# Up half of the expert super-blocks by seven block products in place of eight, with weight sums on VectorE

## What is computed

```python
def expert_block(args):
    xb, e = args
    hid = jax.nn.silu(xb @ w_gate[e]) * (xb @ w_up[e])
    return hid @ w_down[e]
```

## Time and profile before

| | |
|---|---|
| timed runs | 1322.66, 1323.9, 1325.47 us; median 1323.9 us |
| span of the profiled execution, first to last instruction | 1321.3 us |
| TensorE busy | 1299.1 us, 98% of the span |
| VectorE busy | 360.1 us, 27% |
| DMA | 442.52 MB, mean 335 GB/s over the span |
| the item loop | from 444 to 1313 us |
| one item | 108.5 us |

### The profile page before, as it was taken

The page is one execution under the profiler, slowest core; times in us unless marked ns, Lnnn a source line. Parts: engine busy times, 40 slices in busy tenths (PEclk is TensorE's granted clock), DMA queues, the critical chain, the costliest instruction groups (busy, mean ns, idle before and its releaser), DMA issues.

```text
span 1321.3 us, 32549 instructions
## 1 busy us (share of the span) xinstructions
PE 1299.1 (98%) x14662; PEld 879.8 (67%) x14662; DVE 360.1 (27%) x539; ACT 246.4 (19%) x370; POOL 56.0 (4%) x50
## 2 busy tenths in 40 slices
PE   8999999999899999999999999999999999999998
PEld 8998899988767533555745655665574575566565
DVE  5875555554875401000000100100100010010011
ACT  5554544443743100000000000000000000000000
POOL 1001000000000320000000000000000000001600
PEclk9999999999999899999999999999999999999999
DMA  9866555565522899999999999999999999999992
GB/s 321 269 210 225 185 182 177 187 223 191 184 96 72 360 421 420 415 419 418 416 419 419 418 418 418 418 410 419 419 404 420 418 407 418 416 409 414 419 413 110
DMA packets 114199, 442.52 MB, mean 335 GB/s; under 512 B 9284, under 2 KB 55700, under 8 KB 83348
## 3 DMA queue, kind: packets, MB, share of 16 engines
q1 hardware_dynamic: 107904, 424.75, 81.5%
q10 hardware_dynamic: 4820, 11.53, 2.5%
q0 software_dynamic: 1344, 4.20, 0.8%
HBM read 434.12 MB, written 12.08 MB: 338 GB/s over the span
## 4 chain that ended last, share of the span: by engine, by line
PE 93%; DVE 3%; ACT 2%; issue 1%; DMA 0%; ACTq 0%; DVEq 0%
PE bank L1888 44%; PE bank L1900 22%; PE bank L1442 8%; PE bank L1444 8%; PE bank L1443 8%; PE bank L1689 1%; PE bank L1600 1%; DVE w_lo L916 1%; ACT w_hi L626 0%; PE bank L1865 0%; DMA const<-in_shape_constants 0%; ACT ht_hi L654 0%; PE bank L1744 0%; PE bank L1940 0%; DVE q_from L1100 0%
## 5 line engine op out<-in xcount | busy, mean ns | idle before, releaser
L1888 PE MATMUL bank<-more_ring,xT 128*32 128x512 f32 (+1 forms) x3456 | 341.0, 545 | 0.0
L1888 PEld LDWEIGHTS bank<-more_ring,xT 128*32 128x32 f32 x3456 | 164.2, 110 | 163.5 <-issue 84.4
L1888 PE MATMUL bank<-raw,xT 128*32 128x384 f32 (+1 forms) x2688 | 259.3, 532 | 0.7 <-DVE xT L1352 0.7
L1888 PEld LDWEIGHTS bank<-raw,xT 128*32 128x32 f32 x2688 | 122.4, 110 | 127.0 <-issue 76.6
L1411 DVE TENSOR_TENSOR e_hid<-e_silu,bank 128x384 f32<-128x384 f32 (+1 forms) x48 | 26.9, 616 | 542.3 <-PE bank L1888 542.3
L1900 PE MATMUL bank<-more_ring,hidT 128*32 128x256 f32 x3072 | 171.4, 379 | 0.0
L916 DVE TENSOR_TENSOR w_lo<-raw,w_hi 128x2048 fp32r<-128x2048 f32 x62 | 141.5, 2289 | 99.1 <-ACT w_hi L626 99.0
L1900 PEld LDWEIGHTS bank<-more_ring,hidT 128*32 128x32 f32 x3072 | 120.8, 110 | 46.4
L1442 PE MATMUL bank<-ht_hi,w_hi 128*128 128x256 f32 x464 | 129.4, 279 | 1.5 <-DVE ht_lo L930 1.5
L1900 PE MATMUL bank<-raw,hidT 128*32 128x256 f32 x2304 | 129.9, 379 | 0.0
L1444 PE MATMUL bank<-ht_hi,w_lo 128*128 128x256 f32 x464 | 128.9, 278 | 0.0
(11 more groups left out here) (284 smaller groups left out, 898.6 us busy)
## 6 DMA issues: line engine op xcount, KB each, us to landing
more_ring<-in_moe_w_up SPq DMA_DIRECT2D x64, 1024.0 KB, 16.2
more_ring<-in_moe_w_down SPq DMA_DIRECT2D x64, 1024.0 KB, 16.9
raw<-in_moe_w_gate SPq DMA_DIRECT2D x64, 768.0 KB, 15.5
more_ring<-in_moe_w_up SPq DMA_DIRECT2D x64, 768.0 KB, 15.8
raw<-in_moe_w_gate SPq DMA_DIRECT2D x48, 1024.0 KB, 16.1
raw<-in_moe_w_down SPq DMA_DIRECT2D x48, 1024.0 KB, 17.5
more_ring<-in_moe_w_gate SPq DMA_DIRECT2D x16, 1024.0 KB
raw<-in_hgrn_w_in SPq DMA_DIRECT2D x15, 1024.0 KB, 11.8
```

Source lines behind the costliest of these rows:

```text
L1888: ins = nc.tensor.matmul(out_banks[j][GTOK * c:GTOK * c + GTOK, 0:w], xT[:, j, kt, :], chunk[:, c], start=kt == 0, stop=kt == KT - 1)
```

## The change

For token groups 0 and 1 the up half of both super-blocks is computed in pairs of loads (k, k+1). With the token groups as block rows, the two loads as inner blocks and each load's columns cut in half, a pair is a 2 x 2 by 2 x 2 block product. It is formed by seven block products in place of eight: two take token and weight blocks as they are, one takes a token sum and a weight block, one a token block and a weight sum, and three take sums of both. Group 2 is computed as before, in two column halves. The token sums (`token_sums`) and the weight sums (`weight_sums`: four VectorE subtractions of 128 x 768 or 128 x 1024 for each pair) are new, as are the additions that put the seven partial results together (`up_columns`). The products need banks 3 to 7, so the down sums move to banks 1 and 2, where the next item's gate sums of groups 1 and 2 also stand: TensorE therefore begins an item with three loads' products of group 0 and waits for the copies of the last item's result before the other groups. `up_used` now counts a pair of up loads as one step, and `wait_used` and GpSimd's spreads go by that. The early results are fetched into `xs` and a new tile, since `early`'s place now holds the weight sums.

The core of the diff:

```diff
+FAST = (True, True)
...
+            def token_sums(done):
+
+                a11, a12, a21, a22 = (xT[:, j, k:KT:2, :] for j in range(2) for k in range(2))
+                s1, s2, s3, s4 = (xsum[:, i, :, :] for i in range(4))
+                nc.vector.tensor_tensor(s1, a21, a22, ADD).then_inc(xsum_ready, 1)
+                nc.vector.tensor_tensor(s3, a11, a21, SUB).then_inc(xsum_ready, 1)
...
+            def weight_sums(n, sup, pair):
...
+                nc.vector.tensor_tensor(t1, b12, b11, SUB).then_inc(sum_ready, 1)
+                free(2)
+                nc.vector.tensor_tensor(t3, b22, b12, SUB).then_inc(sum_ready, 1)
+                free(3)
+                dve.wait_ge(sum_ready, n * T_STEPS + (done + 1))
+                nc.vector.tensor_tensor(t2, b22, t1, SUB).then_inc(sum_ready, 1)
+                if pair:
+                    dve.wait_ge(up_used, n * UP_STEPS + (PHASE_END[2 * sup] + pair))
+                dve.wait_ge(sum_ready, n * T_STEPS + (done + 3))
+                nc.vector.tensor_tensor(t4, t2, b21, SUB).then_inc(sum_ready, 1)
+            def up_columns(n, sup):
...
+                nc.vector.tensor_tensor(s2, s1, piece("P6", b), ADD).then_inc(part_ready, 1)
+                nc.vector.tensor_tensor(e_hid[:, 0, lo], s1, piece("P2", b), ADD).then_inc(part_ready, 1)
...
+                    act.wait_ge(up_used, n * UP_STEPS + PHASE_END[2 * sup + 1])
+                    nc.scalar.activation(up_part[:, 0, 0:w // 2], piece("P1", w // 2), ACT.Copy).then_inc(first_copied, 1)
...
-                nc.scalar.activation(yb[:, 0:512], banks[6][0:CAP, :], ACT.Copy)
+                nc.scalar.activation(yb[:, 0:512], banks[1][0:CAP, :], ACT.Copy)
...
+            def fast_products(n, sup, pair):
...
+                def times(name, rows, columns, begin=True):
+                    dst, opens = piece(name, b), PLACES[name][2] and begin and pair == 0
+                    for c in range(4):
+                        ins = nc.tensor.matmul(dst[GTOK * c:GTOK * c + GTOK, :], rows, columns[:, c], start=opens,
+                                               stop=pair == PAIRS - 1, skip_group_check=True)
+                    return ins
+
+                times("P1", xT[:, 0, k, :], b11)
+                times("P2", xT[:, 0, k + 1, :], b21)
+                if pair == 0:
+                    pe.wait_ge(xsum_ready, n * 4 + 4)
+                times("P3", xsum[:, 3, pair, :], b22)
+                times("H1", xT[:, 2, k, :], b11)
+                times("H1", xT[:, 2, k + 1, :], b21, False)
+                times("H2", xT[:, 2, k, :], b12)
+                times("H2", xT[:, 2, k + 1, :], b22, False)
+                pe.wait_ge(sum_ready, n * T_STEPS + (done + 1))
+                times("P5", xsum[:, 0, pair, :], t1).then_inc(sum_used, 1)
+                pe.wait_ge(sum_ready, n * T_STEPS + (done + 2))
+                times("P7", xsum[:, 2, pair, :], t3).then_inc(sum_used, 1)
+                pe.wait_ge(sum_ready, n * T_STEPS + (done + 3))
+                times("P6", xsum[:, 1, pair, :], t2).then_inc(sum_used, 1)
+                pe.wait_ge(sum_ready, n * T_STEPS + (done + 4))
+                times("P4", xT[:, 1, k + 1, :], t4).then_inc(up_used, 1)
...
-                            ins = nc.tensor.matmul(banks[6 + j // 2][GTOK * c:GTOK * c + GTOK, 256 * (j % 2):256 * (j % 2) + 256],
+                            ins = nc.tensor.matmul(banks[1 + j // 2][GTOK * c:GTOK * c + GTOK, 256 * (j % 2):256 * (j % 2) + 256],
...
+                        for kt in range(AHEAD):
+                            loaded(kt)
+                            up_products(banks, kt, w, (0,))
+                        pe.wait_ge(yb_ready, n * 2 + 1)
+                        for kt in range(AHEAD):
+                            up_products(banks, kt, w, (1, 2))
+                        plain = range(AHEAD, KT)
...
+                    if FAST[sup]:
+                        for pair in range(PAIRS):
+                            loaded(i + 2 * pair)
+                            loaded(i + 2 * pair + 1)
+                            fast_products(n, sup, pair)
...
-                        pe.wait_ge(yb_ready, n * 2 + 1)
+                        pe.wait_ge(e_silu_ready, n * (2 * GRPS) + 2 * GRPS)
```

More of the change, by code:

```diff
@@ L49 @@
 SIGNALS = N_LOADS // 2
+FAST = (True, True)
+UP_USED, PHASE_END = [], []
+for _sup in range(2):
+    for _half in range(2):
+        _done = PHASE_END[-1] if PHASE_END else 0
+        _step = 2 if _half and FAST[_sup] else 1
+        UP_USED += [_done + kt // _step + 1 for kt in range(KT)]
+        PHASE_END.append(_done + KT // _step)
+UP_STEPS = PHASE_END[-1]
+PAIRS = KT // 2
+AHEAD = 3
+FAST_BEFORE = (0, PAIRS if FAST[0] else 0)
+T_STEPS = 4 * PAIRS * sum(FAST)
 def ring_offset(k):
@@ L153, in build_program @@
         with ExitStack() as over:
-            early = sb(over, "early", [P, TT, 2, D])
+            sums = sb(over, "sums", [P, 4, 4 * 256])
         ht_hi = sb(ctx, "ht_hi", [P, KT, T], f32r)
@@ L161, in build_program @@
         cols = sb(ctx, "cols", [P, 64])
+        with ExitStack() as over:
+            up_part = sb(over, "up_part", [P, 2, 256])
+            xsum = sb(over, "xsum", [P, 4, PAIRS, GTOK])
         gain_row = sb(ctx, "gain_row", [P, D])
@@ L251, in build_program @@
         s = ExitStack()
+        early_second = sb(ctx, "early_second", [P, TT, D])
         e_silu = sb(s, "e_silu", [P, GRPS, 512])
@@ L423, in build_program, with piece @@
         LO_FFN, LO_KV, LO_Q = 4, 8, 12
-        END_BANKS = [banks[1], banks[2], banks[5], banks[0]]
+        END_BANKS = [banks[3], banks[4], banks[5], banks[6]]
+        early = [xs[:, :, :], early_second[:, :, :]]
+        PLACES = {"P1": (3, 0, True), "P2": (3, 1, False), "P3": (4, 0, True), "H1": (5, 0, True), "H2": (5, 1, False),
+                  "P5": (4, 1, False), "P7": (6, 0, True), "P6": (6, 1, False), "P4": (7, 0, True)}
+        def piece(name, width):
+            bank, half, _ = PLACES[name]
+            return banks[bank][:, width * half:width * half + width]
         TURN0 = TURN_ATT
@@ L599, in _ @@
                     at = bass.IndirectOffsetOnAxis(ap=early_slot[:, t, i:i + 1], axis=0)
-                    nc.gpsimd.indirect_dma_start(out=early[:, t, i, :], out_offset=None, in_=slot_rows, in_offset=at).then_inc(fetched[t][i], 16)
+                    nc.gpsimd.indirect_dma_start(out=early[i][:, t, :], out_offset=None, in_=slot_rows, in_offset=at).then_inc(fetched[t][i], 16)
             for i in range(2):
@@ L603, in _ @@
                     pool.wait_ge(fetched[t][i], 16)
-                    rows = early[:, t, i, :]
+                    rows = early[i][:, t, :]
                     then(nc.gpsimd.tensor_scalar(rows, rows, gate[:, t, i:i + 1], None, MUL))
@@ L1407, in _ @@
                 for sup, (_, w) in enumerate(SUPERS):
[L1408 to L1411 removed]
+                    if FAST[sup]:
+                        for pair in range(PAIRS):
+                            weight_sums(n, sup, pair)
+                        up_columns(n, sup)
+                    else:
+                        dve.wait_ge(up_used, n * UP_STEPS + PHASE_END[2 * sup + 1])
+                        for j in range(GRPS):
+                            dve.wait_ge(e_silu_ready, n * (2 * GRPS) + (GRPS * sup + j + 1))
+                            nc.vector.tensor_tensor(e_hid[:, j, 0:w], e_silu[:, j, 0:w], banks[GRPS + j][:, 0:w], MUL).then_inc(e_hid_ready, 1)
                     dve.wait_ge(e_hid_ready, n * (2 * GRPS) + (GRPS * sup + GRPS))
@@ L1880, in _, with by_strip, up_products @@
                 gather(1, j)
-            def up_products(out_banks, i, w):
+            def by_strip(columns):
+                return columns.rearrange("p (m c i) -> p c m i", c=4, i=2 * GTOK)
+            def up_products(out_banks, i, w, groups=range(GRPS)):
                 kt = i % KT
-                chunk = ring_place(i).rearrange("p (m c i) -> p c m i", c=4, i=2 * GTOK)
-                for j in range(GRPS):
+                chunk = by_strip(ring_place(i))
+                for j in groups:
                     for c in range(4):
@@ L1889, in up_products @@
                                                chunk[:, c], start=kt == 0, stop=kt == KT - 1)
-                ins.then_inc(up_used, 1)
+                if GRPS - 1 in groups:
+                    ins.then_inc(up_used, 1)
+            def fast_products(n, sup, pair):
+                w = SUPERS[sup][1]
+                b, k = w // 2, 2 * pair
+                first = 2 * KT * sup + KT + k
+                done = 4 * (FAST_BEFORE[sup] + pair)
+                (b11, b12), (b21, b22) = ((by_strip(ring_place(i)[:, 0:2 * w]), by_strip(ring_place(i)[:, 2 * w:4 * w]))
+                                          for i in (first, first + 1))
+                t1, t2, t3, t4 = (by_strip(sums[:, i, 0:2 * w]) for i in range(4))
+                def times(name, rows, columns, begin=True):
[21 more added lines that the diff above has]
```

(1 more changed line is left out.)

87 lines of the change are left out of this document (69 added, 18 removed).

## The result

| | before | after |
|---|---|---|
| median of 14 runs | 1323.63 us | 1329.34 us |
| span of the profiled execution | 1321.3 us | 1326.6 us |

The ratio is 1.0037, 95% interval 1.0027 to 1.0047: slower by 0.37%, where 1316.6 us was forecast. The ratio leaves out one run of the kernel before, 1371.61 us, that stands far from all the others.

The account below looks back on a forecast made before the run. TensorE and the DMA engines are both full: TensorE would save 22.6 us, but the loads leave 9.4 to spare, less 2.1 for instruction fetches, a gain of 7.3: 1323.9 - 7.3 = 1316.6 us, range 1311 to 1326.

Parts of the forecast that it names:

- Products: Up half: shorter bursts save 1.20 us an item in super-block 0 and 1.63 in super-block 1, 22.6 for eight items.
- The 192-column burst: Super-block 0's up half: a burst takes 0.162 us; a rival, chance 0.06, said 0.216 and 1339 us.
- VectorE's sums: Four weight sums a pair in the up half: 0.95 us each at 768 elements, 1.22 at 1024, costed at nothing.
- So VectorE keeps up, barely: Super-block 0's pairs: sums take 3.60 us against 3.57 of products, costed nothing; rival of VectorE as bound 0.08, 1338 us.
- There is also more to fetch.: Instruction fetches on the DMA engines: 5600 more instructions, 21 packets, make the last load land 2.1 us later.
- The rival of small losses at the joints: At the item's joints: small losses eat the gain; chance 0.09.
- The wait at an item's start: Item's head: group 0's three loads hide the wait for result copies; uncovered it costs 0.3 us an item, 2.4 in all.
- The loads as the next bound: TensorE waits for loads from about the sixth item, the last landing at 1302.7; chance 0.62, 1313 to 1320 us.
- the spare: End of the last item: TensorE reaches the last load 9.4 us after it landed, all that the transfers leave.
- 1302, the rival: Whole loop: transfers are no bound, so the gain is 22.6 us less small change, time 1302; chance 0.06.
- with its products right behind: End of the last item: the last load lands at 1300 to 1304 and TensorE's products on it follow at once.
- The clock: Last three items: waits for loads lower TensorE's clock, up to 10 us, about half regained, 1321.5 us; chance 0.09.

Follow-up runs that it names:

- e13_group2_whole: Changed kernel with super-block 0's third token group in whole 384-column bursts, GpSimd's early-result work held back, loop head at slot 90 in place of 128: 1320.0 us.
- e10_slot96: Changed kernel with GpSimd's early-result work held until the last item's up half is over and the loop head at slot 96 in place of 128: 1333.0 us.
- e8_no_products: Changed kernel without the seven products and weight sums (eight products kept in both super-blocks), the rest of the change kept: 1324.3 us.
- e9_slot64: Changed kernel with GpSimd's early-result work held until the last item's up half is over and the loop head at slot 64 in place of 128: 1343.1 us.
- e5_slot218: Changed kernel with GpSimd's early-result work held until the last item's up half is over and the loop head at slot 218 in place of 128: 1365.1 us.
- e2_late_early: Changed kernel with GpSimd's scaling and adding of early results put behind the last item's up products, loop head still at slot 128: 1323.9 us.

## Why the prediction was wrong

- **Products: right.** U1 takes the forecast 18.99 us, U0 14.26 where nothing holds it (`e13_group2_whole`, in part in wider bursts) and 14.30 to 14.34 in three items of `e10_slot96`. The 192-column burst costs 0.162 us, not 0.216. The Trainium skill ("TensorE: Matmul & The Clock Gate", section "Wait — 56ns, not 53.3ns?") gives 25 ns from start to start; the trace does not agree. Matmuls of one burst, which go to different strips, start 6 to 7 ns apart, and matmuls and weight loads counted together come 8 in 0.162 us, 20 ns each; matmuls alone come every 40 ns on average.
- **VectorE's sums: right in size, but not free.** Rows of after, for the earlier trace rows:

```profile
L1475 DVE TENSOR_TENSOR sums<-more_ring 128x1024 f32<-128x1024 f32 x32 | 39.0, 1218 | 0.0
L1473 DVE TENSOR_TENSOR sums<-more_ring 128x768 f32<-128x768 f32 x32 | 30.5, 955 | 121.0 <-PE bank L2021 102.7 <-DMA more_ring<-in_moe_w_up 16.9 <-issue 1.4
L1478 DVE TENSOR_TENSOR sums<-more_ring,sums 128x768 f32<-128x768 f32 x32 | 33.5, 1046 | 0.0
```

  0.95 and 1.22 us were forecast. The 1046 is the last item's, where GpSimd works beside it. "So VectorE keeps up, barely" did not quite hold: in U0 of items 2 to 7 the second pair's fourth sum ends 7.13 us into the stage, its product starts at 7.18, and in the items of `e10_slot96` that take 14.3 us it starts at 6.82. That is 0.36 us an item, 2.2 of the 2.8 us of the table, a wait for VectorE that was put at nothing. VectorE begins that pair 0.6 us later there, since P5's last matmul comes later; why is open. The sum in the third item, whose product starts at 685.12:

```profile
684.10 0.96 DVE L1482 TENSOR_TENSOR sums<-sums,more_ring 128x768 f32<-128x768 f32 x1
```

  For the last item, the prediction knew of the early results only as a transfer and of VectorE's lack of slack (0.03 us a pair), and did not put the two together: 5.5 to 6 us, the waits for instructions and the clock behind them included. The Trainium skill ("SBUF — State Buffer", section "SBUF: two separate sides") says that an instruction of VectorE with two inputs in the buffer and one of GpSimd that reads it exclude each other for their whole length. The sum that ended 0.8 us after GpSimd's addition agrees with it. Other sums do not show it so plainly: beside one scaling of GpSimd (1230.67 to 1234.50) two sums took 0.95 us and one 1.79.
- **The failed step: "There is also more to fetch."** The prediction priced 5600 more instructions as 21 packets on the DMA engines, 2.1 us. The packets came nearly as counted, 24 more, and took 0.7% of the DMA engines in place of 0.6. What cost was TensorE standing still for instructions, a term that the prediction did not have: 14.0 us at the branch, 2.8 in the last U0, and some 2 in G0, where a gap of 0.1 to 0.4 us ends 2.3 to 2.6 us after a packet's start. The 2.5 us of the first U0 lie in several small gaps that no packet explains; they stay open. The rival of small losses at the joints named the place, with a chance of 0.09, and no mechanism. The Trainium skill ("Runtime: NRT & Kernel Launch", section "Instruction fetch mechanics") calls the cost of passing into the next block mostly hidden, and warns of a stall for a taken branch whose target is not at hand. The trace agrees with the warning (0.45 us or up to 4.4, by the place of the branch), and disagrees with "mostly hidden" for the narrow stage: it asks for 49 instructions a microsecond (8 in 0.162 us), and starved it got 42.
- **The wait at an item's start: right.** `e8_no_products` has it and is level with before.
- **The loads as the next bound: right, but not reached.** In the changed kernel the stalls ate the spare before the loads could. Where they are gone, items take 105.6 us (105.7 forecast), waits for loads begin at the sixth item (sixth), the last load lands at 1302.9 (1302.7, so near partly by luck: the 2.1 us in it were a choice between 1.4 and 2.8) and the time is 1320.0 (1316.6). Without the bound it is 1304.5 (1302, the rival). What failed of it is "with its products right behind": the waits came at the up loads, and TensorE reached the last load's products at about 1305.5, 2.6 us after it had landed. VectorE's sums behind each late up load are a likely part of that; it was not tried.
- **The clock: a small part.** It fell after some long stalls, not after the waits for loads (0.3 to 1.7 us). In `e9_slot64` a head gap was followed by 0.64 of the granted clock, between 1.2 and 2.4 GHz; the same gap in another item left it at 1.00:

```profile
555.50:560.10 4.60, 4.44 (x36) 1.69 (x40) 1.50 (x2) 0.00 (x0) 0.00 (x0) 0.64 1.02 418
...
780.30:784.90 4.60, 4.47 (x56) 1.92 (x60) 1.55 (x2) 0.00 (x0) 0.00 (x0) 1.00 1.02 418
```

  In the last item of the changed kernel it stood at 0.72 from 1236.4 to 1241.5, behind the 2.77 us; some 1.9 us of that U0 are of this kind (20.9 less the 14.7 of other items and the waits of 1.5 and 2.8).

What stays open: why the narrow stage stalls in some items and not in others of one run (`e10_slot96`: 14.3 us in three, 16.1 to 18.3 in five), and whether the cure in `e13_group2_whole` is the lower density alone or also where its blocks begin; the two were changed together. Its 40 instructions a microsecond lie just under the 42 of the estimate.

## What to carry to other kernels

Instructions of a loop body are a supply with a price of its own. Before a change makes it longer or denser, look at the closing branch's time and at "issue" waits in the profile, and count where the longer body puts the branch in its block; one constant for the loop's place moved the same body here from 1324 to 1365 us. Where an engine gets new work beside a bound one without slack, list what the other engines run at the same moment, also in the first and the last pass of the loop. And when TensorE and the loads are both full, a saving on one is worth only the spare of the other: half a change (super-block 1 alone) took all that was to be had.

## What was not expected of the hardware

- The branch that closes the loop took 0.36 to 4.4 us a turn by its place in a block of 256 instructions, on a straight line of 0.028 us a slot.
- `e5_slot218` and `e2_late_early` differ in the slot alone and stand at 1365.1 and 1323.9 us, 3.1% apart.
- TensorE ran dry in the middle of a straight stretch, without a branch, when it issued some 49 instructions a microsecond (8 in 0.162 us); at 37 no such gap was over 0.35 us, and at 40 (the narrow stage of `e13_group2_whole`) there was none from the second item on.
- A wait for instructions ended 2.5 us after the start of a packet of 16.4 KB, at a branch and in the middle of a stage alike, and in the starved narrow stage blocks came 6.1 us apart at the closest.
